# Moving two weight preparations around a layer norm in a transformer kernel on one core

## The chip, the cores and the metric

One NeuronCore of one Trainium2 chip runs the whole program. TensorE multiplies matrices into eight PSUM banks, VectorE and ScalarE evict, normalise and prepare, GpSimd does some additions and small transfers, SyncE issues the large loads. The metric is the device time of one execution in microseconds; the times given are medians of several executions.

## The reference

Three transformer layers over 512 tokens of width 1024, in float32. The first has its own form; the other two, which matter here, are

```python
def hybrid_layer(x, w_in, w_out, w_ff1, w_ff2, ...):
    proj = x @ w_in                      # queries, keys, values of two attentions, a gate
    ...                                  # forgetting attention, retention with group norm
    mix = jnp.einsum('bsc,cd->bsd', mixed, w_out)
    x = layernorm(DEEPNORM_ALPHA * x + mix, ln1_g, ln1_b)
    hid = jnp.square(jax.nn.relu(jnp.einsum('bsd,df->bsf', x, w_ff1)))
    ff = jnp.einsum('bsf,fd->bsd', hid, w_ff2)
    return layernorm(DEEPNORM_ALPHA * x + ff, ln2_g, ln2_b)
```

The layer norm needs the mean and the variance of all 1024 channels of a token, that is, all eight output tiles of `w_out` or `w_ff2`, before the first matmul of the next stage has an operand.

## The kernel before, in words

Activations lie transposed: 8 tiles of 128 channels by 512 tokens (`H`, and `P` and `Q` as operands). Each float32 operand is held as a high and a low part (`Phi`, `Plo`, `Qhi`, `Qlo` and for weights `wh`, `wl`, in further slots `wxh`, `wxl`), and each product takes three passes of TensorE: high by high (L710), high by low (L711), low by high (L713).

**Weights.** A weight matrix comes in slabs of 1 MB (SyncE, L2929) that land in two staging buffers by turns, and each slab is cut into pieces, here two of 128 output columns. Slab n may be loaded once the pieces of slab n-2 have been cut. To *prepare* a piece is one ScalarE copy to the high part (L2203, it waits for the slab to land) and one VectorE subtraction for the low part (L1301, it waits for ScalarE). Both stand in the instruction queues of these engines in program order, between evictions and norm work, so where they are placed decides what they hold up. A piece needs one of seven slots while the kernel is `wide` (four otherwise); a slot is free again when TensorE has used its piece.

The class `Walk` is run by every engine alike, so that all agree on the order. `piece(ahead, more)` takes the next piece and prepares others in advance:

```python
most = max(self.prepared + 1 + (i + 1) % 2, i + 1) + more
while self.prepared < min(i + (ahead or self.ahead) + more, len(self.weights.pieces), most) and self.ready():
    self.prepare(behind=self.behind)
```

`prepare(True)` does the high half at once and returns the low half as a function to call later.

**The stage around the change.** Behind attention and retention the output projection runs: tiles 0 and 1 together (`w.two`), 2 to 4 one by one (`w.gemm`), each evicted by VectorE into `H` (L1787, L1790), added to a running sum `accq` (L1814), and reduced by a preliminary centre `cB` (L1824), squared by ScalarE (L2586) and summed into `acc2` (L1836). Then `last_three` takes tiles 5, 6 and 7 in two halves of 256 tokens, so that the norm of the first half runs beside the matmuls of the second. Its order on TensorE: `part(0..2, 0)`, five of the eight steps of `part(0, 1)`, `mean(N, 0)` (L1038, a matmul with ones that waits for `accq` behind tile 7's first half, L1846), the rest of `part(0, 1)`, `scale(N, 0)` (L1048), `part(1, 1)`, `part(2, 1)`, and then `head`: the first four output tiles of the next stage, which need the low parts of the normalised operand (L1900). VectorE's order is written out by hand to match: per tile and half an eviction (L1859, L1862), a sum (L1846), a deviation (L1824), squares added (L1836), then `mean` (L1873), `minus` (L1880), `variance` (L1886), `times` (L1893, it needs ScalarE's reciprocal root L2610, L2612) and `lows` (L1900), in between. ScalarE has the squares, `mean` (L2603, L2605), the root, and the final scaling (L2621) with the high part (L2626).

`last_three` is called with N = 0 and N = 2 behind the output projections of the two layers, with N = 1 and N = 3 behind their feed-forward parts; the last has no next stage. It holds two places at which weights are prepared: one ahead of the third tail tile, up to three pieces in advance of use, and `fourth`, whose high half stands behind `mean(0)` and (on VectorE) `minus(0, 0, 1, 2, 3)`, and whose low half stands ahead of `times(0, 0)`.

Of the kernel before, what the change touches and what calls it, by code (L numbers as in the profile page):

```python
# [24 lines left out]
ALPHA = float(4 ** 0.25)  # L25
# [488 lines left out]
def build(nc, xT, w_in, gate_up, w_bm, w_bg, w_out, w_up, w_down, w_in2, w_out2, w_ff1, w_ff2,  # L514
          consts, params, out, vrev, cneg):
    ctx = ExitStack()
    with ctx:
# [5 lines left out]
        def signal(name):  # L523
            return Signal(ctx.enter_context(nc.semaphore(name)))
# [3 lines left out]
        w_low, vec_x, vec_attn, vec_gla, vec_ret, vec_norm = DVE = [  # L528
            signal(f"s_dve_{n}") for n in ("weight_low", "tile", "attention", "gla", "retention", "norm")]
# [163 lines left out]
        def tensor(e):  # L693
            on = Waits(e)
            w = Walk(weights, PE)
# [3 lines left out]
            def tile(hi_x, lo_x, ready):  # L699

                def step(i, c, b, k, nk, kx=None, tok=WHOLE):
                    kx = k if kx is None else kx
                    _, hi, lo = weights.tiles(i, stage, wh, wl, w.slot[i])
                    cs_ = slice(128 * c, min(128 * c + 128, weights.width(i)))
                    o = banks[b][0:cs_.stop - cs_.start, tok]
                    if k == 0:
                        on.wait_ge(w_high[i], *ready(kx), *free[b])
                    else:
                        on.wait_ge(w_high[i], *ready(kx))
                    e.matmul(o, hi[:, k, cs_], hi_x[:, kx, tok], start=k == 0, stop=False)  # L710
                    e.matmul(o, hi[:, k, cs_], lo_x[:, kx, tok], start=False, stop=False)  # L711
                    on.wait_ge(w_low[i])
                    t = e.matmul(o, lo[:, k, cs_], hi_x[:, kx, tok], start=False, stop=k == nk - 1)  # L713
                    if k == nk - 1:
                        t.then_inc(*(gemm.up("tile", i, c) if tok is WHOLE else gemm.up("half", i, tok.start // 256)))
                return step
# [63 lines left out]
            def frees(*events):  # L780

                def evict(i, c, b):
                    free[b] = [s[key + (i, c)] for s, key in events]
                return evict
# [245 lines left out]
            def norm_tile(N, j):  # L1030
                if j == 1:
                    w.beside.append(spaced([lambda: centre(N)], 3))
                    w.pace = 1.0
# [21 lines left out]
            def last_three(N, F, nxt, last_wide=False):  # L1055
                tail = [w.piece(1) for _ in range(3)]
                low = [w.next_bank() for _ in range(3)]
                high = [w.next_bank(), 6, 7]
                Q_ = tile(Qhi, Qlo, lambda k: [vec_x["hidden", F, 3, k] if N % 2 else vec_x["Q", "out", N, k]])

                def part(p, hf, ks):
                    b = (low, high)[hf][p]
                    for k in ks:
                        Q_(tail[p], 0, b, k, 8, tok=HALVES[hf])
                    if ks[-1] == 7:
                        free[b] = [vec_x["late", N, 5 + p, hf]]
                        if hf:
                            w.read_by["Q"] = tail[p]
                            w.release(tail[p])

                for _ in range(3 if nxt else 0):
                    if w.prepared < w.used + 3:
                        w.prepare()
                part(0, 0, range(8))
                part(1, 0, range(8))
                while nxt and w.prepared < w.used + 3:
                    w.prepare()
                part(2, 0, range(8))
                part(0, 1, range(5))
                mean(N, 0, (7, 0))  # L1080
                fourth = w.prepare(True) if nxt else None
                if last_wide:
                    w.narrow()
                part(0, 1, (5, 6, 7))
                scale(N, 0, (7, 0))
                if not nxt:
                    part(1, 1, range(8))
                    part(2, 1, range(8))
                    mean(N, 1, (6, 1), rest=7)
                    scale(N, 1, (6, 1), rest=7)  # L1090
                    return
                if fourth:
                    fourth()
                part(1, 1, range(8))
                part(2, 1, range(8))
                gemm.mark(("tail", N))
                four = [(w.piece(1), w.next_bank()) for _ in range(4)]

                def head(hf, ks):
                    P_ = tile(Phi, Plo, lambda k: [vec_norm["low", N, k, hf]])  # L1100
                    for k in ks:
                        for i, b in four:
                            P_(i, 0, b, k, 8, tok=HALVES[hf])

                head(0, (0, 1))
                mean(N, 1, (7, 1))
                head(0, (2, 3))
                scale(N, 1, (7, 1))
                head(0, (4, 5, 6, 7))
                w.prepare()  # L1110
                w.prepare()
                head(1, range(4))
                P_ = tile(Phi, Plo, lambda k: [vec_norm["low", N, k, 1]])
                for (i, b), ev in zip(four, nxt):
                    for k in range(4, 8):
                        P_(i, 0, b, k, 8, tok=HALVES[1])
                    gemm.mark(("tile", i, 0))
                    w.read_by["P"] = i
                    w.release(i)
                    if not last_wide or ev in nxt[:2]:  # L1120
                        ev(i, 0, b)
                for ((i, b), ev) in list(zip(four, nxt if last_wide else ()))[2:]:
                    ev(i, 0, b)
                return tile(Phi, Plo, lambda k: [vec_norm["low", N, k, 0], vec_norm["low", N, k, 1]])
# [3 lines left out]
            for L in range(2):  # L1128
# [137 lines left out]
                Qo = tile(Qhi, Qlo, lambda k: [vec_x["Q", "out", N, k]])  # L1266
# [2 lines left out]
                norm_tile(N, 0)  # L1269
                norm_tile(N, 1)  # L1270
                for j in range(2, 5):
                    w.gemm("Q", 8, Qo, frees((vec_x, ("ev",))), more=int(j == 4))
                    norm_tile(N, j)
                w.mark("hidden", F)
                Pn = last_three(N, F, [frees((act_x, ("up", F)))] * 4)
# [16 lines left out]
        def vector(e):  # L1292
# [20 lines left out]
            w = Walk(weights, DVE, low=low, sums=weight_sums)  # L1313
# [469 lines left out]
            def ev_down(j, scale=None, *events):  # L1783
                def evict(i, c, b):
                    on.wait_ge(gemm["tile", i, c], *h_over[j])
                    if scale:
                        t = e.scalar_tensor_tensor(out=H[:, j, :], in0=H[:, j, :], scalar=scale, in1=banks[b][:, :],  # L1787
                                                   op0=ALU.mult, op1=ALU.add)
                    else:
                        t = e.tensor_tensor(H[:, j, :], H[:, j, :], banks[b][:, :], ALU.add)  # L1790
                    t.then_inc(*vec_x.up("ev", i, c))
                    h_over[j] = [vec_x["ev", i, c]]
                return evict
# [56 lines left out]
            def last_three(N, F, scale, nxt, last_wide=False):  # L1850
# [54 lines left out]
                        w.prepare()  # L1905
                part(0, 0)
                part(1, 0)
                while nxt and w.prepared < w.used + 3:
                    w.prepare()
                part(2, 0)  # L1910
                add_squares(N)
                mean(0)
                minus(0, 0, 1, 2, 3)
                fourth = w.prepare(True) if nxt else None
                if last_wide:
                    w.narrow()
                part(0, 1)
# [1 line left out]
                if not nxt:  # L1919
# [18 lines left out]
                                        prm[:, V_LN2B + 14:V_LN2B + 15], ALU.mult, ALU.add)  # L1938
                    t.then_inc(*vec_norm.up("final", N, 6, 1))
                    return  # L1940
                if fourth:
                    fourth()
                times(0, 0)
                minus(0, 4)
                times(0, 1)
# [45 lines left out]
            for L in range(2):  # L1991
# [187 lines left out]
                norm_tile(N, 0)  # L2179
                norm_tile(N, 1)  # L2180
                for j in range(2, 5):
                    w.gemm("Q", 8, nothing, ev_down(j, ALPHA), more=int(j == 4))
                    norm_tile(N, j)
                w.mark("hidden", F)
                last_three(N, F, ALPHA, [ev_up(F, 0, j) for j in range(4)])
# [7 lines left out]
        def scalar(e):  # L2193
# [17 lines left out]
            w = Walk(weights, SCA, high=high)  # L2211
# [273 lines left out]
            def ev_down(j):  # L2485
                def evict(i, c, b):
                    h_over[j] = [vec_x["ev", i, c]]
                return evict
# [100 lines left out]
            def last_three(N, F, nxt, last_wide=False):  # L2589
# [4 lines left out]
                def part(p, hf):  # L2594
                    if hf:
                        w.read_by["Q"] = tail[p]
                        w.release(tail[p])
                    deviate(N, 5 + p, hf)
# [32 lines left out]
                        w.prepare()  # L2631
                part(0, 0)
                part(1, 0)
                while nxt and w.prepared < w.used + 3:
                    w.prepare()
                part(2, 0)
                mean(0)
                fourth = w.prepare(True) if nxt else None
                if last_wide:
                    w.narrow()  # L2640
                part(0, 1)
# [1 line left out]
                if not nxt:  # L2643
# [6 lines left out]
                    times(0, 5, 6, 7)  # L2650
                    times(1, 0, 1, 2, 3, 4, 5, 7)
                    return
                if fourth:
                    fourth()
                times(0, 0, 1)
                part(1, 1)
                times(0, 2)
# [21 lines left out]
            for L in range(2):  # L2679
# [131 lines left out]
                norm_tile(N, 0)  # L2811
                norm_tile(N, 1)
                for j in range(2, 5):
                    w.gemm("Q", 8, nothing, ev_down(j), more=int(j == 4))
                    norm_tile(N, j)
                w.mark("hidden", F)
                last_three(N, F, [ev_up(F, 0, j) for j in range(4)])
# [215 lines left out]
```

## Time and profile before

| | us |
|---|---|
| median of 3 runs | 2037.71 (2037.26 to 2037.96) |
| the profiled execution | 2037.82 |
| its span, first to last instruction | 2036.0 |
| TensorE busy with matmuls | 2009.3 (99%) |
| VectorE busy | 1327.5 (65%) |
| ScalarE busy | 1023.7 (50%) |
| GpSimd busy | 367.6 (18%) |
| mean granted TensorE clock | 0.998 |

The profile records one execution. Busy time counts every instruction in flight; TensorE's matmuls overlap, so 99% busy says that it seldom waited, not that it did peak work. A timeline row gives start, duration, engine, line, operation, what was written and read, the count of instructions merged into it, and in brackets how long the engine had been idle before it and which instruction released it. In the notes on SyncE's queue a load's time runs from its issue to its landing.

### The profile page before, as it was taken

Reading aid. Unit: us, or ns where it says so; the run is one execution under the profiler, and the core shown is the slowest. Engines: PE = TensorE matmul, PEld = TensorE weight load, DVE = VectorE, ACT = ScalarE, POOL = GpSimd, SP = SyncE. Lnnn points to the kernel's source line nnn. Section 1 sums busy time; section 2 is a strip of 40 time slices with the busy share of each in tenths; the row PEclk is TensorE's granted clock in tenths of the full one; section 3 lists DMA queues with packets and bytes.
Section 4 is the critical chain, followed back from the end, with each engine's and each line's share of the span. In section 5 each row is a group of like instructions: output and inputs, shape, how many; then the busy total and the mean of one; then the engine's idle time right before and its main releaser. Section 6 shows DMA issues by size and latency. Waiting matters only on the chain.

```text
span 2036.0 us, 27794 instructions
## 1 busy us (share of the span) xinstructions
PE 2009.3 (99%) x11032; PEld 1730.4 (85%) x11032; DVE 1327.5 (65%) x2095; ACT 1023.7 (50%) x1688; POOL 367.6 (18%) x315
## 2 busy tenths in 40 slices
PE   9999999999999999999999999999999999999997
PEld 6888888888898998888778899898888788899896
DVE  6765666556774665577677675567676687566576
ACT  6664344334362543466357364454566357354363
POOL 0010000000223230354000233130353000323220
PEclk9999999999999999999999999999999999999999
DMA  8332213333332323633332242332542332242431
GB/s 246 99 109 64 83 63 104 124 104 103 100 107 84 124 75 92 186 107 85 118 96 89 77 145 62 104 119 69 166 116 87 119 101 86 66 142 62 125 104 42
DMA packets 201534, 211.58 MB, mean 104 GB/s; under 512 B 7804, under 2 KB 181116, under 8 KB 201405
## 3 DMA queue, kind: packets, MB, share of 16 engines
q1 hardware_dynamic: 194544, 194.13, 30.6%
q0 software_dynamic: 6352, 15.24, 2.9%
q8 instruction: 87, 1.43, 0.3%
q10 hardware_dynamic: 508, 0.43, 0.1%
q14 instruction: 43, 0.34, 0.1%
HBM read 194.55 MB, written 8.95 MB: 100 GB/s over the span
## 4 chain that ended last, share of the span: by engine, by line
PE 90%; DVE 5%; ACT 2%; DMA 1%; issue 1%; SPq 0%; DVEq 0%; ACTq 0%
PE ps L710 19%; PE ps L713 19%; PE ps L711 19%; PE ps L766 6%; PE ps L764 6%; PE ps L762 6%; PE ps L735 2%; PE ps L738 2%; PE ps L736 2%; PE ps L817 1%; PE ps L808 1%; DVE d L1880 1%; PE ps L1227 1%; PE ps L1242 1%; PE ps L799 1%
## 5 line engine op out<-in xcount | busy, mean ns | idle before, releaser
L710 PE MATMUL ps<-Phi,wh 128*128 128x512 f32 (+1 forms) x888 | 347.4, 391 | 2.9 <-DVE Plo L1322 1.3
L1301 DVE TENSOR_TENSOR wl<-stage,wh 128x1024 fp32r<-128x1024 f32 (+1 forms) x246 | 310.4, 1267 | 37.0 <-ACT wh L2203 34.7
L713 PE MATMUL ps<-Phi,wl 128*128 128x512 f32 (+1 forms) x888 | 331.9, 374 | 0.6 <-DVE wl L1301 0.6
L711 PE MATMUL ps<-Plo,wh 128*128 128x512 f32 (+1 forms) x888 | 331.3, 373 | 0.0
L2203 ACT ACTIVATE wh<-stage 128x1024 fp32r<-128x1024 f32 (+3 forms) x249 | 248.2, 1009 | 65.5 <-PE ps L713 40.1
L710 PE MATMUL ps<-Qhi,wh 128*128 128x512 f32 (+1 forms) x664 | 252.1, 380 | 0.0
L713 PE MATMUL ps<-Qhi,wl 128*128 128x512 f32 (+1 forms) x664 | 251.8, 379 | 0.0
L711 PE MATMUL ps<-Qlo,wh 128*128 128x512 f32 (+1 forms) x664 | 251.6, 379 | 0.0
L2838 POOL TENSOR_TENSOR ws<-stage 128x1024 f32<-128x1024 f32 x20 | 55.0, 2751 | 923.1 <-PE ps L713 442.8
L710 PEld LDWEIGHTS ps<-Phi,wh 128*128 128x128 f32 x888 | 167.7, 189 | 34.3 <-DVE Plo L1900 5.1
L713 PEld LDWEIGHTS ps<-Phi,wl 128*128 128x128 f32 x888 | 167.2, 188 | 31.7 <-DVE wl L1301 1.0
L711 PEld LDWEIGHTS ps<-Plo,wh 128*128 128x128 f32 x888 | 167.8, 189 | 25.6 <-issue 1.2
L1790 DVE TENSOR_TENSOR H<-H,ps 128x512 f32<-128x512 f32 x74 | 50.8, 687 | 173.4 <-PE ps L713 173.4
L710 PE MATMUL ps<-Qhi,wxh 128*128 128x512 f32 (+1 forms) x424 | 152.5, 360 | 0.0
L711 PE MATMUL ps<-Qlo,wxh 128*128 128x512 f32 (+1 forms) x424 | 151.4, 357 | 0.0
L713 PE MATMUL ps<-Qhi,wxl 128*128 128x512 f32 (+1 forms) x424 | 151.3, 357 | 0.0
L713 PEld LDWEIGHTS ps<-Qhi,wl 128*128 128x128 f32 x664 | 124.9, 188 | 24.2 <-DVE wl L1301 0.8
L710 PEld LDWEIGHTS ps<-Qhi,wh 128*128 128x128 f32 x664 | 124.9, 188 | 23.7 <-DVE Qlo L1320 0.5
L711 PEld LDWEIGHTS ps<-Qlo,wh 128*128 128x128 f32 x664 | 124.9, 188 | 23.4
L1320 DVE TENSOR_TENSOR Qlo<-f,Qhi 128x512 fp32r<-128x512 f32 x96 | 82.3, 857 | 68.6 <-ACT Qhi L2220 68.6
L1301 DVE TENSOR_TENSOR wxl<-stage,wxh 128x1024 fp32r<-128x1024 f32 (+1 forms) x90 | 115.1, 1283 | 8.4 <-ACT wxh L2203 8.3
L2203 ACT ACTIVATE wxh<-stage 128x1024 fp32r<-128x1024 f32 (+1 forms) x90 | 85.4, 965 | 38.9 <-PE ps L713 21.7
(375 smaller groups left out, 4600.4 us busy)
## 6 DMA issues: line engine op xcount, KB each, us to landing
stage<-in_w_ff SPq DMA_DIRECT2D x64, 1024.0 KB, 5.4
stage<-in_w_in SPq DMA_DIRECT2D x39, 1024.0 KB, 5.1
stage<-in_w_up SPq DMA_DIRECT2D x16, 1024.0 KB, 5.5
stage<-in_w_down SPq DMA_DIRECT2D x16, 1024.0 KB, 4.9
stage<-in_w_in SPq DMA_DIRECT2D x30, 512.0 KB, 5.2
stage<-in_w_out SPq DMA_DIRECT2D x12, 1024.0 KB, 4.9
stage<-in_w_bg SPq DMA_DIRECT2D x4, 1024.0 KB, 4.9
vrev<-H SPq DMA_DIRECT2D x2, 2048.0 KB, 14.7
```

The costliest lines, as they stand in the source:

```text
L710: e.matmul(o, hi[:, k, cs_], hi_x[:, kx, tok], start=k == 0, stop=False)
L711: e.matmul(o, hi[:, k, cs_], lo_x[:, kx, tok], start=False, stop=False)
L713: t = e.matmul(o, lo[:, k, cs_], hi_x[:, kx, tok], start=False, stop=k == nk - 1)
L735: e.matmul(o, hi_x[:, kk, sl], hi[:, k, :], start=kk == 0, stop=False)
L762: e.matmul(o, hi[:, k0 + k, :], x, start=k == 0 and name not in again, stop=False, skip_group_check=name in again)
L764: e.matmul(o, hi[:, k0 + k, :], y, start=False, stop=False, skip_group_check=name in again)
L766: t = e.matmul(o, lo[:, k0 + k, :], x, start=False, stop=k == 3, skip_group_check=name in again)
L1301: t = e.tensor_tensor(lo, src, hi.bitcast(F32), ALU.subtract)
L1320: t = e.tensor_tensor(lo, src, hi.bitcast(F32), ALU.subtract)
L1790: t = e.tensor_tensor(H[:, j, :], H[:, j, :], banks[b][:, :], ALU.add)
L2203: e.activation(hi, src, ACT.Copy).then_inc(*w_high.up(i))
L2838: e.tensor_tensor(ws[u][:, :, :, :], one, other, ALU.add).then_inc(*pool.up("weights", i))
```

## The change

All three engines' copies of the program are changed alike. In `last_three` the weights ahead of the third tail tile are prepared up to four in advance instead of three, and `fourth` goes. In the loop over output tiles 2 to 4 behind retention, `more` is 1 for tiles 2 and 4 instead of for tile 4 alone. The diff of TensorE's copy:

```diff
@@ last_three
                 part(1, 0, range(8))
-                while nxt and w.prepared < w.used + 3:
+                while nxt and w.prepared < w.used + 4:
                     w.prepare()
                 part(2, 0, range(8))
                 part(0, 1, range(5))
                 mean(N, 0, (7, 0))
-                fourth = w.prepare(True) if nxt else None
                 if last_wide:
                     w.narrow()
...
-                if fourth:
-                    fourth()
                 part(1, 1, range(8))
...
@@ behind retention
                 for j in range(2, 5):
-                    w.gemm("Q", 8, Qo, frees((vec_x, ("ev",))), more=int(j == 4))
+                    w.gemm("Q", 8, Qo, frees((vec_x, ("ev",))), more=int(j != 3))
                     norm_tile(N, j)
```

VectorE's copy (from L1905, L1914, L1941 and L2182) and ScalarE's (from L2631, L2638, L2653 and L2814), where the same lines stand among other calls:

```diff
                 part(1, 0)
-                while nxt and w.prepared < w.used + 3:
+                while nxt and w.prepared < w.used + 4:
                     w.prepare()
                 part(2, 0)
                 add_squares(N)
                 mean(0)
                 minus(0, 0, 1, 2, 3)
-                fourth = w.prepare(True) if nxt else None
...
-                if fourth:
-                    fourth()
                 times(0, 0)
```

TensorE's copy prepares nothing itself; there the calls only keep count.

## Rows read from the trace of the kernel before

**Rows 1.** The page: busy time, share of the span and instructions of each engine.

```profile
PE 2009.3 (99%) x11032; PEld 1730.4 (85%) x11032; DVE 1327.5 (65%) x2095; ACT 1023.7 (50%) x1688; POOL 367.6 (18%) x315
```

**Rows 2.** Timeline of VectorE, place A: start us, us, what, [idle time before, releaser].

```profile
1039.17 1.23 DVE L1301 TENSOR_TENSOR wxl<-stage,wxh 128x1024 fp32r<-128x1024 f32 x1 [1.58 <-ACT wxh L2203]
...
1043.97 1.22 DVE L1301 TENSOR_TENSOR wl<-stage,wh 128x1024 fp32r<-128x1024 f32 x1 [1.65 <-ACT wh L2203]
...
1049.45 2.36 DVE L1301 TENSOR_TENSOR wl<-stage,wh 128x1024 fp32r<-128x1024 f32 x2
1053.80 1.23 DVE L1301 TENSOR_TENSOR wl<-stage,wh 128x1024 fp32r<-128x1024 f32 x1 [1.99 <-ACT wh L2203]
1054.94 0.68 DVE L1787 SCALAR_TENSOR_TENSOR H<-H,ps 128x512 f32<-128x512 f32 x1
...
1062.22 0.41 DVE L1859 SCALAR_TENSOR_TENSOR H<-H,ps 128x256 f32<-128x256 f32 x1
...
1067.44 1.22 DVE L1301 TENSOR_TENSOR wxl<-stage,wxh 128x1024 fp32r<-128x1024 f32 x1
```

**Rows 3.** Timeline of ScalarE, place A.

```profile
1052.64 1.06 ACT L2203 ACTIVATE wh<-stage 128x1024 fp32r<-128x1024 f32 x1 [2.35 <-DMA stage<-in_w_ff]
...
1061.43 0.42 ACT L2586 ACTIVATE sq<-d 128x256 f32<-128x256 f32 x1 [0.71 <-DVE d L1824]
...
1064.76 0.42 ACT L2605 ACTIVATE qB<-qB 128x256 f32<-128x256 f32 x1 [0.49 <-DVE qB L1873]
1065.08 1.05 ACT L2203 ACTIVATE wxh<-stage 128x1024 fp32r<-128x1024 f32 x1
...
1068.10 0.42 ACT L2612 ACTIVATE rB<-tB 128x256 f32<-128x256 f32 x1
```

**Rows 4.** Timeline of TensorE, place A: first half's mean, next stage's first matmul.

```profile
1063.14 0.70 PE L1038 MATMUL ps<-accq,onec 128*128 128x256 f32 x2 [2.68 <-DVE accq L1846]
...
1071.23 0.36 PE L710 MATMUL ps<-Phi,wh 128*128 128x256 f32 x1
```

**Rows 5.** SyncE's queue; loads issued in 1045:1046, 1641:1642, 1653:1654, us to landing.

```profile
1641.44 0.37 SPq L2929 DMA_DIRECT2D stage<-in_w_out  x1
...
stage<-in_w_ff SPq DMA_DIRECT2D x1, 1024.0 KB, 7.3
...
stage<-in_w_out SPq DMA_DIRECT2D x1, 1024.0 KB, 5.1
...
stage<-in_w_ff SPq DMA_DIRECT2D x1, 1024.0 KB, 5.3
```

**Rows 6.** Timeline of ScalarE, place B: square of tile 6's first half.

```profile
1405.46 0.42 ACT L2586 ACTIVATE sq<-d 128x256 f32<-128x256 f32 x1 [0.71 <-DVE d L1824]
```

**Rows 7.** Timeline of VectorE, place B: eviction of tile 7's first half.

```profile
1406.50 0.42 DVE L1862 TENSOR_TENSOR H<-H,ps 128x256 f32<-128x256 f32 x1 [0.16 <-PE ps L713]
```

**Rows 8.** Timeline of TensorE, place B: mean, next stage's first matmul.

```profile
1408.10 0.60 PE L1038 MATMUL ps<-accq,onec 128*128 128x256 f32 x2
...
1416.08 0.35 PE L710 MATMUL ps<-Phi,wh 128*128 128x256 f32 x1
```

**Rows 9.** Timeline of VectorE, place C.

```profile
1647.50 0.69 DVE L1787 SCALAR_TENSOR_TENSOR H<-H,ps 128x512 f32<-128x512 f32 x1 [1.60 <-PE ps L713]
...
1652.38 1.22 DVE L1301 TENSOR_TENSOR wl<-stage,wh 128x1024 fp32r<-128x1024 f32 x1
...
1657.84 2.36 DVE L1301 TENSOR_TENSOR wl<-stage,wh 128x1024 fp32r<-128x1024 f32 x2
...
1664.44 1.23 DVE L1301 TENSOR_TENSOR wl<-stage,wh 128x1024 fp32r<-128x1024 f32 x1
...
1668.75 0.41 DVE L1859 SCALAR_TENSOR_TENSOR H<-H,ps 128x256 f32<-128x256 f32 x1
```

**Rows 10.** Windows: PE, PEld, DVE, ACT, POOL busy (x), PEclk, DMA share, GB/s.

```profile
1063.00:1068.00 5.00, 4.86 (x37) 4.75 (x38) 4.49 (x13) 2.95 (x6) 0.00 (x0) 1.00 0.02 5
2028.00:2030.00 2.00, 0.00 (x0) 0.00 (x0) 2.00 (x8) 2.00 (x5) 0.00 (x0) 0.50 0.11 38
```

More of the change, by code:

```diff
@@ L2181, in vector @@
                 for j in range(2, 5):
-                    w.gemm("Q", 8, nothing, ev_down(j, ALPHA), more=int(j == 4))
+                    w.gemm("Q", 8, nothing, ev_down(j, ALPHA), more=int(j != 3))
                     norm_tile(N, j)
@@ L2633, in last_three @@
                 part(1, 0)
-                while nxt and w.prepared < w.used + 3:
+                while nxt and w.prepared < w.used + 4:
                     w.prepare()
@@ L2637, in last_three @@
                 mean(0)
-                fourth = w.prepare(True) if nxt else None
                 if last_wide:
@@ L2652, in last_three @@
                     return
-                if fourth:
-                    fourth()
                 times(0, 0, 1)
@@ L2813, in scalar @@
                 for j in range(2, 5):
-                    w.gemm("Q", 8, nothing, ev_down(j), more=int(j == 4))
+                    w.gemm("Q", 8, nothing, ev_down(j), more=int(j != 3))
                     norm_tile(N, j)
```

## The prediction, made before the changed kernel was run

> **What bounds the kernel now.** The page comes first: TensorE has a matmul in flight for 99% of the span [rows 1], so a weight that is cut into its halves a little earlier or later only counts where TensorE waits for it, or for something behind it. The timelines of the three places that the diff touches follow, engine by engine. They are the layer norms behind the output projection of layer 0 ("place A", 1030 to 1090 us), behind its feed-forward part ("place B", 1400 to 1436) and behind the output projection of layer 1 ("place C", 1640 to 1700). The piece numbers below count from the first piece of the output projection, 0; 5, 6 and 7 are the last three output tiles, 8 to 11 the four weights of the next stage.
>
> At A VectorE runs one long queue without rest, and what one item waits for all later ones wait for. At the fourth-last tile (j=4) it subtracts pieces 8 and 9 (the x2 row at 1049.45), then idles 1.99 us for ScalarE's high half of piece 10, and only then evicts tile 4 at 1054.94 [rows 2]. ScalarE in turn sat 2.35 us waiting for that slab to land [rows 3]. TensorE pays for it: its mean of the first half waits 2.68 us for the sum that VectorE makes right behind the eviction of tile 7's first half at 1062.22 [rows 4]. From that eviction to the next stage's first matmul pass 9.01 us (1062.22 to 1071.23) in which VectorE is hardly ever idle, so at A TensorE runs at VectorE's pace.
>
> **The change, part by part.** *Which piece goes where.* `piece()` prepares up to one piece, or two where the next piece is even, plus `more`. At A the first piece is even: j=2, 3, 4 prepare 2, 1, 3 pieces now, and 3, 1, 2 after. At C it is odd: 1, 2, 2 and one more ahead of the tail now, and 2, 2, 2 after. At both places, and at B, piece 11 moves: its high half from behind `mean(0)` and its low half from ahead of `times(0, 0)` to a spot between the second and the third tail tile. No instruction is added or removed: each low half stays 1.22 us, 1.14 us from start to the next start (1053.80 to 1054.94) [rows 2].
>
> *Place A, up to the tail.* Piece 7 joins piece 6 at j=2. Its slab is there (piece 6, of the same slab, starts at 1039.17), so evictions, sums and deviations of tiles 2 and 3 all slide by 1.14 us; TensorE doesn't wait for those, its banks come free late in any case. The slab of pieces 10 and 11 is requested when piece 7's low half ends. That was 1043.97 + 1.22 = 1045.2; it becomes 1039.17 + 1.14 + 1.22 = 1041.5, so even with the 7.3 us that this load took [rows 5] it has landed by 1048.8, before the queue reaches it. The two subtractions at j=4 then start at 1049.45 + 1.14 = 1050.59 and the eviction of tile 4 follows at 1052.87 instead of 1054.94: **2.07 us earlier**. The requests keep their order in SyncE's queue, so this one moves past nothing; GpSimd prepares no weights in these stretches.
>
> *Piece 11 in its new spot.* No row of before shows it there, so I build it from its neighbours. ScalarE makes the high half right behind the square of tile 6's first half; from a square to a high half behind it are 0.32 us (1064.76 to 1065.08), the high half takes 1.05 [rows 3], VectorE starts 0.10 after its end (1052.64 + 1.06 to 1053.80) and the next item comes 1.14 later. Sum: tile 7's eviction comes 2.61 us after the start of that square. Now it is 0.79 (1061.43 to 1062.22). The price in VectorE's queue is **1.82 us**, of which 0.7 is idle time. Bounds: 0 if another stall covered it, 1.14 if the high half were ready, 1.82 as built; not more, as the other 0.79 is there now. I take 1.82, since the order in ScalarE's queue forces it. Behind piece 11 the next slab's request is freed some 6 us sooner; its pieces are only cut behind the whole norm, so it is worth nothing. What is given back at the old spot is almost nothing: there the subtraction ended (its next start is 1067.44 + 1.14 = 1068.58) just as ScalarE's reciprocal root became ready (1068.10 + 0.42 = 1068.52), and `times(0, 0)` needs that root [rows 2, 3]. The moved work was free where it stood; without it VectorE idles a microsecond there.
>
> So A: -2.07 + 1.82 = **-0.25 us**; the wait at the mean falls from 2.68 to about 2.4.
>
> *Place B.* Nothing ahead of the tail changes, only piece 11 moves. Its slab landed long before. Square at 1405.46 [rows 6] + 2.61 = 1408.07 against 1406.50 now [rows 7]: +1.57. TensorE reaches its mean at 1408.10 without a wait [rows 8]; the sum would be ready for it 0.92 us behind the eviction (1062.22 to 1063.14 at A) [rows 2, 4], now 1407.42, after 1408.99. A wait of 0.9 us appears. Next stage's first matmul: 1408.07 + 9.01 = 1417.08 against 1416.08: **+1.0 us**. The cover of 0.57 us (9.58 us between the two now, against 9.01) is used up.
>
> *Place C.* Piece 6 moves to j=2. Its slab was requested at 1641.44 and takes 5.1 us [rows 5]: landed 1646.5, high half until 1647.6, low half, next item at 1648.8, where tile 2's eviction stands at 1647.50 now [rows 9]. VectorE's queue is late by 1.3 us from there on (the 1.60 us that it idles for TensorE before this row doesn't cover it, the slab comes too late). The slab of pieces 10 and 11 is requested at the end of piece 7's low half, 1652.38 + 1.22 = 1653.6; after the change that piece is the first of its pair at j=3 rather than the second of its pair now (1.14 sooner), in a queue that is 1.3 us late: the same instant within 0.2. With the 5.3 us that it took [rows 5] it lands at about 1659.1 and pieces 9 and 10 follow each other at j=4 without a gap. In return the subtraction at 1664.44 [rows 9], ahead of the tail, is gone: -1.14 and some 0.2 of hand-over. Net -0.05. Then piece 11: +1.82, tile 7's eviction at 1670.5 instead of 1668.75. C: **+1.75 us**, all of it as a longer wait for the mean.
>
> *Sum.* -0.25 + 1.0 + 1.75 = +2.5 us. The profiled execution took 2037.82 us (span 2036.0), 0.1 above the median of the three runs, 2037.71. I expect a span of 2038.5 and a median of **2040.2 us**, 0.12% more. A difference under 0.2% (4.1 us) is what a measurement of this kernel can't tell from none. Everything behind each place moves rigidly, as TensorE is the bound there.
>
> **Rivals.** *Faster: the stall goes and the insertion is free.* The 1.99 us stall at A is real [rows 2], and if piece 11's insertion found cover (VectorE ahead of TensorE at the third tail tile) A gives 2.07, B nothing (1407.42 is ahead of 1408.10), and C nothing or 0.05: 2035.6 us. Against it: at A and C VectorE is what TensorE waits for at just that point. The Trainium skill (DMA: Bandwidth & Descriptors, section Rules for kernel authors) advises to issue a DMA early and to wait on its semaphore late; by that rule alone this rival would hold. At A the trace agrees for the load, whose landing cost 1.99 us; but the time is then spent in VectorE's queue, of which the rule says nothing. Chance 0.12.
>
> *In between:* piece 11 costs only its 1.14 us at each place (2.0 us less in all: 2038.2), or C's 1.3 us are absorbed (2038.9), or both (2036.9). For it: the 1.60 us of idle time at C. Against it: the order of ScalarE's queue. Chance 0.18, at 2038.5.
>
> *Slower by over 0.2%: a late landing at C.* There piece 10 has no slack: its request isn't earlier, but it is wanted at j=4 rather than ahead of the tail. If that slab takes 7.3 us, as the corresponding one at A did [rows 5], it lands at 1661.0, the high half ends at 1662.0 and the low half starts at 1662.1, where 1657.84 + 1.3 + 1.14 = 1660.3 is forecast [rows 9]: all behind it is 1.8 us later, 2042.0 us. It decides from a load of some 5.5 us on. For it: one of the three loads in [rows 5] was that slow. Against it: that load was at A. Chance 0.10.
>
> *The clock.* With a late landing TensorE's wait at C would be 3.5 us longer than now. After the 2.68 us wait at A the granted clock in the window 1063 to 1068 is 1.00, the 2.4 GHz level; at the end, where TensorE has no more work, it is 0.50 [rows 10]. If it fell at C, the stretch from the mean to the next stage, 8.1 us at A (1063.14 to 1071.23) [rows 4], could take up to twice as long: up to 2050 us. The Trainium skill (TensorE: Matmul & The Clock Gate, HAM oscillation) warns that gaps between bursts of matmuls return the array to its slow clock; the trace agrees only for the end of the kernel, not for the gap at A. Chance 0.02.
>
> That the change does nothing: the same piece would have to find no free slot at its new spot; tile 4's slot is free by then. The loop would not end otherwise. No chance worth a number.
>
> **How the numbers follow.** Forecast 0.58, in between 0.18, faster rival 0.12, late landing 0.10, clock 0.02. All but the last two lie within 0.2% of 2037.71 (2033.6 to 2041.8). Faster by over 0.2% needs more than all of A's wait and C's together: 0.02. Within: 0.87. Slower: 0.11. The forecast's own range is 2039 to 2041.5. The range 2035.5 to 2042.3 takes in the in-between cases (from 2036.9), the faster rival (2035.6), since without it and the late landing 0.24 would be left out, and the late landing (2042.0); only the clock and what nobody thought of stay out.
>
> **What would show it.** Right: at A no idle time of VectorE for ScalarE's high half at j=4, a mean's wait of about 2.4 us; at B a new wait of 0.9 us at the mean; at C a wait there 1.75 us longer than now; VectorE idle for some 0.7 us ahead of piece 11's low half and for a microsecond ahead of `times(0, 0)`, three times each. Wrong: a wait at A under 1 us (insertion covered), none at B, or at C an idle VectorE that waits for a landing.

## The result, and the profile after

| | before | after |
|---|---|---|
| median of 21 runs, us | 2037.60 (2035.79 to 2038.44) | **2040.83** (2039.91 to 2042.57) |
| profiled execution, us | 2037.82 | 2040.88 |
| its span, us | 2036.0 | 2039.1 |
| mean granted TensorE clock | 0.998 | 0.997 |

The ratio is 1.0016, 95% interval 1.0011 to 1.0022: 3.2 us more, within the 0.2% that was called no change, and 0.6 us above the forecast of 2040.2. The executed work is the same; TensorE's share of busy time is again 99% and doesn't show where the time went. The profile's line of busy times, which answers to [rows 1]:

```profile
PE 2010.6 (99%) x11032; PEld 1731.6 (85%) x11032; DVE 1327.4 (65%) x2095; ACT 1023.6 (50%) x1688; POOL 367.1 (18%) x315
```

The waits of TensorE that end on VectorE's sum `accq` (us in total, times, longest), first before, then after:

```profile
PE ps L1038 <- DVE accq L1846: 3.6, 2, 2.7
```

```profile
PE ps L1038 <- DVE accq L1843: 5.7, 3, 2.7
```

Two waits became three. Before, they were 2.68 us at A [rows 4] and 0.90 at C, where TensorE's row is

```profile
1669.68 0.70 PE L1038 MATMUL ps<-accq,onec 128*128 128x256 f32 x2 [0.90 <-DVE accq L1846]
```

After, they are 2.38 at A, 0.66 at B and 2.68 at C. Timeline of VectorE after, place A, answering to [rows 2] (three fewer lines stand above it, so L1301 is L1298, L1787 is L1784, L1859 is L1856, L1893 is L1890):

```profile
1039.25 1.22 DVE L1298 TENSOR_TENSOR wxl<-stage,wxh 128x1024 fp32r<-128x1024 f32 x1 [1.62 <-ACT wxh L2197]
1040.39 1.22 DVE L1298 TENSOR_TENSOR wl<-stage,wh 128x1024 fp32r<-128x1024 f32 x1
...
1050.65 2.36 DVE L1298 TENSOR_TENSOR wl<-stage,wh 128x1024 fp32r<-128x1024 f32 x2
1052.93 0.68 DVE L1784 SCALAR_TENSOR_TENSOR H<-H,ps 128x512 f32<-128x512 f32 x1
...
1060.81 1.23 DVE L1298 TENSOR_TENSOR wxl<-stage,wxh 128x1024 fp32r<-128x1024 f32 x1 [0.52 <-ACT wxh L2197]
1061.95 0.41 DVE L1856 SCALAR_TENSOR_TENSOR H<-H,ps 128x256 f32<-128x256 f32 x1
...
1068.29 0.43 DVE L1890 TENSOR_TENSOR d<-d,rB 128x256 f32<-128x256 f32 x1 [1.02 <-ACT rB L2606]
```

Piece 7 follows piece 6 at once, and at j=4 the two subtractions run into the eviction of tile 4 (1052.93, forecast 1052.87) with no idle time: the 1.99 us are gone. Piece 11 stands ahead of tile 7's eviction (1061.95, forecast 1061.97). The last row is the old spot: VectorE now idles there for the root. TensorE's rows at A, answering to [rows 4]: the wait is 0.30 shorter, and the next stage begins 0.29 us sooner (forecast 0.25).

```profile
1062.88 0.70 PE L1038 MATMUL ps<-accq,onec 128*128 128x256 f32 x2 [2.38 <-DVE accq L1843]
...
1070.94 0.36 PE L710 MATMUL ps<-Phi,wh 128*128 128x256 f32 x1
```

Place B, VectorE, answering to [rows 7]:

```profile
1406.54 1.23 DVE L1298 TENSOR_TENSOR wl<-stage,wh 128x1024 fp32r<-128x1024 f32 x1 [0.52 <-ACT wh L2197]
1407.68 0.41 DVE L1859 TENSOR_TENSOR H<-H,ps 128x256 f32<-128x256 f32 x1
```

Place B, TensorE, answering to [rows 8]:

```profile
1408.61 0.70 PE L1038 MATMUL ps<-accq,onec 128*128 128x256 f32 x2 [0.66 <-DVE accq L1843]
...
1416.67 0.35 PE L710 MATMUL ps<-Phi,wh 128*128 128x256 f32 x1
```

The kernel arrives at B 0.3 us early, so in its own time the eviction is 1.18 + 0.3 = 1.5 us later, and the next stage 0.59 + 0.3 = 0.9 us. Place C, VectorE, answering to [rows 9]:

```profile
1648.46 1.23 DVE L1298 TENSOR_TENSOR wxl<-stage,wxh 128x1024 fp32r<-128x1024 f32 x1 [1.74 <-ACT wxh L2197]
1649.60 0.68 DVE L1784 SCALAR_TENSOR_TENSOR H<-H,ps 128x512 f32<-128x512 f32 x1
...
1661.18 1.23 DVE L1298 TENSOR_TENSOR wl<-stage,wh 128x1024 fp32r<-128x1024 f32 x1 [0.17 <-ACT wh L2197]
1662.32 0.68 DVE L1784 SCALAR_TENSOR_TENSOR H<-H,ps 128x512 f32<-128x512 f32 x1
...
1670.20 1.23 DVE L1298 TENSOR_TENSOR wxl<-stage,wxh 128x1024 fp32r<-128x1024 f32 x1 [0.52 <-ACT wxh L2197]
1671.35 0.41 DVE L1856 SCALAR_TENSOR_TENSOR H<-H,ps 128x256 f32<-128x256 f32 x1
...
1673.95 0.42 DVE L1870 TENSOR_TENSOR qB<-muB,cB 128x256 f32<-128x256 f32 x1 [0.49 <-ACT muB L2597]
```

The kernel enters C 0.82 us late. Tile 2's eviction is 1649.60 - 1647.50 - 0.82 = 1.28 us late in its own time (forecast 1.3), tile 7's 1671.35 - 1668.75 - 0.82 = 1.78 (forecast 1.75). VectorE's queue did what was forecast of it. The last row is new: 0.49 us of idle time for `muB`, ScalarE's copy of the mean. Its cause stands in TensorE's rows there:

```profile
1672.27 1.22 PE L1038 MATMUL ps<-accq,onec 128*128 128x256 f32 x2 [2.68 <-DVE accq L1843]
```

The mean takes 1.22 us where it took 0.70 before. The windows around it (PE, PEld, DVE, ACT, POOL, then PEclk, DMA share, GB/s), of after; before, each of them has 1.00:

```profile
1672.00:1673.00 1.00, 0.73 (x3) 0.64 (x3) 0.55 (x2) 0.41 (x1) 0.00 (x0) 0.58 0.35 70
1673.00:1674.00 1.00, 1.00 (x6) 0.91 (x5) 0.48 (x2) 0.39 (x2) 0.00 (x0) 0.50 0.84 201
1674.00:1675.00 1.00, 1.00 (x6) 1.00 (x6) 1.00 (x4) 0.42 (x1) 0.00 (x0) 0.50 0.96 292
1675.00:1676.00 1.00, 1.00 (x6) 0.91 (x6) 1.00 (x4) 0.00 (x0) 0.00 (x0) 0.71 1.09 389
```

TensorE's clock was at its lower level, 1.2 GHz, for some 3.4 us behind the wait; from 1676 on it is 1.00 again. C cost 1.78 + 0.49 = 2.27 us; read from the shifts in the table below it is 2.26.

### The profile page after: what moved, and what is told of

The parts are those of the page before. It is cut to its first block, busy times and chain, and to the rows that moved or that the text cites. A ratio compares the mean times of both kernels' runs of the same rounds, so it can differ in the third digit from the quotient of the medians.

```text
span 2039.1 us, 27794 instructions
## 1 busy us (share of the span) xinstructions
PE 2010.6 (99%) x11032; PEld 1731.6 (85%) x11032; DVE 1327.4 (65%) x2095; ACT 1023.6 (50%) x1688; POOL 367.1 (18%) x315
## 4 chain that ended last, share of the span: by engine, by line
PE 89%; DVE 5%; ACT 3%; DMA 1%; issue 1%; SPq 0%; DVEq 0%; ACTq 0%
PE ps L710 19%; PE ps L713 19%; PE ps L711 19%; PE ps L766 6%; PE ps L764 6%; PE ps L762 6%; PE ps L735 2%; PE ps L738 2%; PE ps L736 2%; PE ps L817 1%; PE ps L808 1%; DVE d L1877 1%; PE ps L1224 1%; PE ps L1239 1%; PE ps L799 1%
## 5 line engine op out<-in xcount | busy, mean ns | idle before, releaser
L1298 DVE TENSOR_TENSOR wl<-stage,wh 128x1024 fp32r<-128x1024 f32 (+1 forms) x246 | 310.1, 1266 | 35.6 <-ACT wh L2197 33.6
L1787 DVE TENSOR_TENSOR H<-H,ps 128x512 f32<-128x512 f32 x74 | 50.8, 686 | 174.9 <-PE ps L713 174.8
L1298 DVE TENSOR_TENSOR wxl<-stage,wxh 128x1024 fp32r<-128x1024 f32 (+1 forms) x90 | 115.1, 1283 | 9.4 <-ACT wxh L2197 9.3
```

The costliest lines, as they stand in the source:

```text
L1298: t = e.tensor_tensor(lo, src, hi.bitcast(F32), ALU.subtract)
```

## The experiments

All kernels but the fillers' one compute the same operations in another order. Where the time is gained and lost is read from ScalarE's rows: the shift of each against the same row of the profiled execution of before, the median of nine in a row, in us. A place costs the difference of two neighbouring columns. The table has all experiments; they follow one by one.

| kernel | median us (runs) | entering A | behind A | behind B | entering C | behind C |
|---|---|---|---|---|---|---|
| the change | 2040.83 (21) | 0.05 | -0.31 | 0.58 | 0.82 | 3.08 |
| e1, extra weight alone | **2036.03** (11) | 0.11 | -1.82 | -1.82 | -1.72 | -1.75 |
| e2, move alone | 2043.52 (8) | -0.14 | 0.16 | 1.06 | 1.07 | 3.33 |
| e3, extra weight in layer 0 | 2036.05 (11) | -0.22 | -2.44 | -2.45 | -1.69 | -1.71 |
| e4, high half sooner | 2039.02 (11) | 0.08 | -0.74 | -0.31 | -0.14 | 0.93 |
| e5, move at B alone | 2038.68 (11) | -0.18 | -0.51 | 0.38 | 0.91 | 0.88 |
| e6, fillers at C | 2040.32 (11) | -0.04 | 0.04 | 0.94 | 1.01 | 2.72 |
| e7, move alone again | 2042.19 (1) | -0.10 | 1.62 | 2.51 | 2.68 | 4.38 |
| e8, before again | 2037.45 (1) | 0.00 | -0.22 | -0.24 | -0.30 | -0.34 |

**e1, the extra weight alone.** From the change, the move undone in all three engines' copies:

```diff
-                while nxt and w.prepared < w.used + 4:
+                while nxt and w.prepared < w.used + 3:
                     w.prepare()
...
+                fourth = w.prepare(True) if nxt else None
...
+                if fourth:
+                    fourth()
```

> One part alone: the weight that is prepared at the third output tile is kept, the move of the fourth is undone (its high half again behind the mean, its low half behind the wait). My theory (the extra piece takes a VectorE stall of 2.07 us away at A, and is worth nothing at C): 2.1 us less than before, about 2035.5 us, the wait of the mean's matmul at A down from 2.68 to about 0.6 us, at B unchanged, at C unchanged or up by at most 0.1, and the clock at C at 1.00. The rival (the extra piece itself makes VectorE late at C, by its 1.3 us behind a slab that lands late, and gives nothing at A): 2037.6 to 2039 us. If both are right at once, A gains 2.1 and C loses 1.3: 2036.8 us.

2036.03 us (2035.38 to 2036.50) against 2037.71 for before beside it; the ratio is 0.9993, interval 0.9984 to 1.0001, so the gain of 1.7 us is at the edge of what this measurement tells from none, though all 11 runs lie below 26 of the 30 of before. The gain is all at A: 1.93 us (0.11 to -1.82). VectorE there:

```profile
1050.86 2.36 DVE L1301 TENSOR_TENSOR wl<-stage,wh 128x1024 fp32r<-128x1024 f32 x2
1053.14 0.68 DVE L1787 SCALAR_TENSOR_TENSOR H<-H,ps 128x512 f32<-128x512 f32 x1
...
1060.41 0.42 DVE L1859 SCALAR_TENSOR_TENSOR H<-H,ps 128x256 f32<-128x256 f32 x1
```

TensorE at A: the wait is 0.77 us instead of 2.68 (0.6 expected).

```profile
1061.34 0.70 PE L1038 MATMUL ps<-accq,onec 128*128 128x256 f32 x2 [0.77 <-DVE accq L1846]
```

At C the kernel loses and wins nothing (-1.72 to -1.75; forecast -0.05), with a wait of 0.89 us and a clock of 1.00. The rival, that the extra weight itself costs at C, falls. From tile 4's to tile 7's eviction are 1060.41 - 1053.14 = 7.27 us here and 1061.95 - 1052.93 = 9.02 with the change: the moved piece costs 1.75 us of VectorE's queue (forecast 1.82).

**e3, the extra weight in layer 0 alone.** As e1, and

```diff
-                    w.gemm("Q", 8, Qo, frees((vec_x, ("ev",))), more=int(j != 3))
+                    w.gemm("Q", 8, Qo, frees((vec_x, ("ev",))), more=int(j == 4 or (L == 0 and j == 2)))
```

> The extra weight at the third output tile in layer 0 alone (place A), the move undone. My theory: A gives 2.07 us and C is as before, so 2035.5 us, the same as with the extra weight in both layers within 0.2 us. The rival (the extra piece costs at C what it is queued behind, 1.3 us): this kernel is 1.1 to 1.3 us faster than the one with it in both layers.

2036.05 us (2035.69 to 2037.00), ratio 0.9992 (0.9984 to 1.0001): the same as e1. A gave 2.22 us here (-0.22 to -2.44), of which 0.76 were lost again between B and C (see e5). The extra weight in layer 1 is worth nothing, and costs nothing.

**e2 and e7, the move alone.** From the change:

```diff
-                    w.gemm("Q", 8, Qo, frees((vec_x, ("ev",))), more=int(j != 3))
+                    w.gemm("Q", 8, Qo, frees((vec_x, ("ev",))), more=int(j == 4))
```

> The other part alone: the fourth is moved ahead of the last tail tile, the extra weight at the third output tile is left out. My theory (the move costs 1.8 us at A, 0.9 at B, 1.8 at C, and the extra piece is what pays A's back): 4.5 us more than before, 2042.1 us, with the wait of the mean's matmul at A at about 4.5 us, at B 0.7, at C 2.7; where the clock falls in a wait, up to 0.5 us more for each such place, so up to 2043.1. The rival (the two parts only work together, the pieces prepared early are what makes the move dear): 2038 to 2039.5 us.

2043.52 us (2041.08 to 2044.96), ratio 1.0027 (1.0017 to 1.0038). The move costs 5.8 us by the medians; 4.5 were expected, up to 1.0 more for the clock. B took 0.90 (0.16 to 1.06) and C 2.26 (1.07 to 3.33), as with the change, so the extra weight has no part in either. But A took only 0.30 in the profiled execution, at 2041.16 us, where 1.8 was expected, and TensorE's wait there was 2.78 us, not 4.5. The runs fell apart into 2 near 2041.1 and 6 from 2042.5 up. So it was profiled once more:

> The kernel with the move alone once more, for its profile: its runs fell into two groups, 2041.1 us (2 of 8) and 2042.5 to 2045.0 (6 of 8), and the execution shown so far is of the first. The theory (the slab of feed-forward weights that is issued at 1045.3 us lands in 5.5 us in the first group and in 7.3 us in the second, as in the kernel before): with 3 chances in 4 a run of 2043 to 2044 us, and then VectorE idle for about 2 us behind the high half at the last full output tile, where the first group has 0.30. The rival (the second group is of the clock alone): a run of the second group has that idle time at 0.3 us and a clock that falls at more places.

It took 2042.19 us, in neither of the two groups, where 2043 to 2044 had been expected with 3 chances in 4. The load of the slab of pieces 10 and 11 (us from issue to landing: least, median, longest), and VectorE's timeline row with what it idled for the high half at j=4. In e2:

```profile
DMA to landing us min/median/max: 5.6/5.6/5.6
```

```profile
1051.99 1.23 DVE L1298 TENSOR_TENSOR wl<-stage,wh 128x1024 fp32r<-128x1024 f32 x1 [0.30 <-ACT wh L2197]
```

In e7:

```profile
DMA to landing us min/median/max: 6.9/6.9/6.9
```

```profile
1053.40 1.23 DVE L1298 TENSOR_TENSOR wl<-stage,wh 128x1024 fp32r<-128x1024 f32 x1 [1.59 <-ACT wh L2197]
```

The stall follows the landing to the tenth: 1.3 us later, 1.29 us more idle time, and A cost 1.72 instead of 0.30. Of the 0.13 that is left, the clock explains about half (0.31 in e7 against 0.25 in e2, by how much more the shift grows between 1055 and 1075 than with the change). The 0.30 of e2 is then the piece's 1.75 and the clock's 0.25, less the 1.69 by which its stall is shorter than the 1.99 of before.

What sets the two groups apart is not shown by this. No execution of the slower one was profiled, and a landing as late as in before (0.4 us more than e7's) and a fall of the clock at C (0.55) would bring e7 to some 2043.1 us, an estimate; five of the eight runs took 2043.42 to 2044.96. Their mean granted clocks are 0.995 and 0.996, against 0.997 and 0.998 in the other three, so the clock has a part in it that no profile here shows.

**e8, the kernel before once more.**

> The kernel before once more, for its profile: 5 of its 30 runs took 2035.9 to 2036.4 us, the others 2037 to 2038.4. The theory (the same slab lands on time in the few and late in the many): a run near 2037.7 us with the slab's landing at 7 us or more and VectorE idle for about 2 us at the last full output tile of A, or a run near 2036.1 us with the landing at 5.5 us and hardly any idle time there. The rival (the groups differ in something else): the landing and the time do not go together.

2037.45 us. That is a run of the many, with a landing and an idle time somewhat below what was expected for it. Its load and VectorE's row, answering to [rows 5] (7.3 us) and [rows 2] (1.99):

```profile
DMA to landing us min/median/max: 6.8/6.8/6.8
```

```profile
1053.39 1.22 DVE L1301 TENSOR_TENSOR wl<-stage,wh 128x1024 fp32r<-128x1024 f32 x1 [1.49 <-ACT wh L2203]
```

Across all executions that have this wait the two go together: 5.6 us and 0.30 (e2), 6.8 and 1.49 (e8), 6.8 and 1.52 (e5), 6.9 and 1.59 (e7), 7.3 and 1.99 (before). That the few shortest runs of before (4 of 30 at 2035.9 to 2036.4; the expectation says 5) are those with a landing in time fits their distance of about 1.5 us from the others, but none of them was profiled, so it is argued and not shown.

**e4, the high half sooner.** From the change, piece 11 between the tail tiles, split over two spots:

```diff
                 part(0, 0)
+                fourth = w.prepare(True) if nxt else None
                 part(1, 0)
-                while nxt and w.prepared < w.used + 4:
-                    w.prepare()
+                if fourth:
+                    fourth()
                 part(2, 0)
```

> The whole change, but the moved fourth is split: its high half is made on ScalarE behind the first tail tile, its low half on VectorE behind the second, so that VectorE no longer idles for the high half between them. My theory (of the 1.8 us that the moved low half costs in VectorE's queue, 1.14 is its own time and 0.7 idle time for the high half): 0.7 us less at A, at B and at C than with the change, so up to 2.1 us less, 2038.7 us; at C the wait of the mean falls to about 2.0 us, and the clock there may stay at 1.00, 0.5 us more. The rival (the idle time comes of ScalarE being behind with its squares anyway): within 0.4 us of the change, 2040.4 to 2041.2 us.

2039.02 us (2038.54 to 2039.45), ratio 1.0007 (0.9998 to 1.0016), so 1.8 us less than the change (up to 2.1 expected). VectorE at A:

```profile
1052.97 0.68 DVE L1785 SCALAR_TENSOR_TENSOR H<-H,ps 128x512 f32<-128x512 f32 x1
...
1060.04 0.43 DVE L1834 TENSOR_TENSOR acc<-acc,sq 128x256 f32<-128x256 f32 x1 [0.28 <-ACT sq L2582]
1060.38 1.22 DVE L1299 TENSOR_TENSOR wxl<-stage,wxh 128x1024 fp32r<-128x1024 f32 x1
1061.52 0.41 DVE L1857 SCALAR_TENSOR_TENSOR H<-H,ps 128x256 f32<-128x256 f32 x1
```

The 0.52 us for the high half are gone, but 0.28 for the square behind it came in their place. It saved 0.46 at A (-0.82 against -0.36), 0.46 at B and 1.19 at C; at C the wait is 2.01 us and the clock stays at 1.00, which is 0.49 of it. So of the 1.75 us some 0.5 to 0.7 came of the order of ScalarE's queue. The rest is the low half itself, and it still isn't worth its place: e1 is 3 us faster.

**e5, the move at B alone**, made from the kernel before:

```diff
-                while nxt and w.prepared < w.used + 3:
+                while nxt and w.prepared < w.used + (4 if N == 1 else 3):
                     w.prepare()
...
-                fourth = w.prepare(True) if nxt else None
+                fourth = w.prepare(True) if nxt and N != 1 else None
```

> The move at one place alone, B, where no extra weight is prepared: the kernel before with the fourth ahead of the last tail tile behind layer 0's feed-forward, and nothing else changed. My theory (1.57 us more in VectorE's queue, a wait of about 0.7 us at the mean's matmul where there was none): 0.9 us more at B, 0.9 to 1.0 us more in the end, 2038.6 us against 2037.7. The rival (what is lost at B is taken back by the slack of layer 1's retention, where VectorE idles for transfers): no difference at the end, within 0.3 us.

2038.68 us (2038.18 to 2039.54) against 2037.72, ratio 1.0005 (0.9996 to 1.0014): 0.96 us by the medians, too little for the interval to tell from none. B itself is read from the trace: 0.89 us (-0.51 to 0.38), with a wait of 0.66. Layer 1's retention doesn't take it back; it added 0.5 of its own, between B and C. There GpSimd waits twice in a row for small transfers, and how long varies from execution to execution. The first of the two waits, in before and in e3:

```profile
1457.68 1.14 POOL L2884 DMA_DIRECT2D x_Cb<-cneg  x2 [3.16 <-DMA cneg<-x_z]
```

```profile
1456.98 1.14 POOL L2884 DMA_DIRECT2D x_Cb<-cneg  x2 [4.91 <-DMA cneg<-x_z]
```

The second, in before and in e5:

```profile
1462.71 0.60 POOL L2900 TENSOR_SCALAR x_bi<-x_Cb,stat 128x128 f32<-128x128 f32 x1 [3.89 <-DMA x_Cb<-cneg]
```

```profile
1463.64 0.60 POOL L2900 TENSOR_SCALAR x_bi<-x_Cb,stat 128x128 f32<-128x128 f32 x1 [4.22 <-DMA x_Cb<-cneg]
```

Both waits together are 7.05 us in before, 7.16 with the change, 7.60 in e5 and 7.73 in e3; between B and C the last three lost 0.24, 0.53 and 0.76 us against before. In the other six executions the sum is 6.98 to 7.13 and the loss -0.06 to 0.17. The two go together, which fits the transfers as the cause, but no run changed the transfers. This also is noise that a single profile brings into such a sum.

**e6, fillers ahead of the mean at C.** The change, with 18 matmuls more whose product is never read:

```diff
+                if N == 2:
+                    on.wait_ge(*free[5])
+                    for _ in range(18):
+                        e.matmul(banks[5][:, 0:256], onecr[:, :], Qhi[:, 0, 0:256], start=True, stop=True)
                 mean(N, 0, (7, 0))
```

> The whole change, with 18 more matmuls of 128 by 256 (about 2.2 us of TensorE, their product is never read) ahead of the mean's matmul at C, so that TensorE does not idle there. The theory (the 2.7 us wait lets the clock fall to 0.5 for 3.4 us, and that costs 0.5 us through the mean, ScalarE's copy of it and VectorE): the granted clock stays at 1.00 from 1665 to 1680 us, muB's row begins 0.4 to 0.5 us earlier behind the mean's last addition, and the time is 0.5 us less than with the change, 2040.3 us. The rival (the clock falls for what TensorE does elsewhere, or its fall is hidden behind VectorE): no difference in time within 0.2 us, or a clock that falls as before.

2040.32 us (2039.90 to 2041.78), 0.51 less than the change; ratio to before 1.0014 (1.0005 to 1.0023). The gap of 0.5 us lies inside the intervals of the two ratios; the trace shows its place. TensorE at C:

```profile
1669.62 2.32 PE L1083 MATMUL ps<-Qhi,onec 128*128 128x256 f32 x18
1672.43 0.70 PE L1038 MATMUL ps<-accq,onec 128*128 128x256 f32 x2 [0.49 <-DVE accq L1847]
```

ScalarE there:

```profile
1673.16 0.39 ACT L2601 ACTIVATE muB<-ps 128x256 f32<-128x256 f32 x1
```

The granted clock is 1.00 from 1664 to 1680, the mean takes 0.70 us, and `muB` comes 0.73 us behind the mean's start, against 1.26 with the change (1672.27 to 1673.53). C cost 1.71 us (1.01 to 2.72), against 2.26. In this same execution the clock fell at A, untouched, and took some 0.2 us.

The experiment does not show that the fillers kept the clock up. In e7 there are none, the wait at C is 2.64 us, and the clock stayed at 1.00 too. What the four executions do show together is the price of the fall: C cost 2.26 in both with it (the change, e2) and 1.70 and 1.71 in both without (e7, e6).

## Why the prediction was right, and where it was off

*What bounds.* Right. The time went into waits of TensorE for VectorE's sum at the three places; between the places the change's shift moves by no more than 0.24 us.

*The stall at A.* Forecast -2.07, shown by e1 as -1.93, by e3 as -2.22 and by the change's eviction of tile 4 as -2.01 (1054.94 to 1052.93). The mechanism was right. What the forecast didn't see is that the stall is no constant of the kernel: it was read from one execution in which the load took 7.3 us, the longest of five. With a load of 5.6 us it is 0.30 us. The extra weight is an insurance against a late landing, not a fixed gain. Beside a run of before that had its slab in time, the 0.3 us that A gained with the change would have been a loss of about 1.3 us (an estimate: 1.99 - 0.30 - 0.36).

*Piece 11's price.* Forecast 1.82 at each place; 1.75 at A, 1.5 in VectorE's queue at B (forecast 1.57), 1.78 net at C (forecast 1.75). The neighbours' rows were enough to build it, though no row showed it. Of the forecast 0.7 us of idle time 0.52 is visible as such, at all three places; at C another 0.15 us stands ahead of the sum of squares before it.

*B's cover.* Forecast +1.0 behind a cover of 0.57; 0.90 with the change, 0.91 in e2, 0.89 in e5. The new wait itself is 0.66 us, where 0.9 was forecast.

*The old spot.* 1.02 us of idle time for the root where the low half had stood, three times, as forecast. The work was free there.

*C.* VectorE's queue as forecast, and the wait went from 0.90 to 2.68 us, 1.78 longer; e1 and e3 show the extra weight's share to be nothing within 0.05. The late landing, the rival on the slower side, was not in this trace: the load took 5.4 us, ScalarE waited 0.26 us for that slab and VectorE 0.17. In all ten profiled executions this load took 5.3 to 5.5 us. Whether the change's three runs at 2042.3 to 2042.6 were late landings was not seen; two of them have the lowest mean clock of the 21, 0.996.

*The step that failed.* The clock. The prediction gave its fall at C a chance of 0.02, and only together with a late landing; it fell with none, behind a wait of 2.68 us, in the one profiled execution of the change, and in one of the two of the move alone. And it was priced at up to 8 us, "up to twice as long" for the stretch from the mean to the next stage. It cost 0.49: the lower level lasted 3.4 us, and in that stretch VectorE sets the pace, so that the slow matmuls held it up only through the one copy `muB`. At 1675.6 TensorE was 4.1 us behind the same matmul of before, at 1684.8 only 3.1. Forecast +2.5, measured in spans +3.1; of the 0.6 between them the clock is 0.49 and the transfers between B and C 0.24, less some 0.2 by which A and B came out better. The Trainium skill (TensorE: Matmul & The Clock Gate, HAM oscillation) warned of gaps between bursts; the trace of the change agrees at C and still not at A.

*The rule on DMA* (the Trainium skill, DMA: Bandwidth & Descriptors, Rules for kernel authors) advises to issue a transfer early and to wait for it late. The runs agree at A: there the load is issued 3.6 us sooner (1041.72 for 1045.30) and the stall is gone, and this is all that helped. e1 is that part without the move, and with e3 it is the fastest kernel here.

## What to carry to other kernels

Preparation that passes from one engine to another belongs where the second one waits anyway, as ahead of `times`, where VectorE waits for the reciprocal root. Moved to a point at which a third engine waits for that queue, as at A and C, it costs its whole length plus the hand-over (1.14 + 0.6 us here), even if its data are there; where there was slack, as at B, it costs what the slack doesn't cover (0.9).

A change made of two parts should be timed as two. Here one gains 1.7 us, and the other costs 4.8 on top of it (2040.83 against 2036.03). Alone it costs 5.8 (2043.52 against 2037.71): the parts don't simply add up, and the missing microsecond is not explained here.

A stall read from one execution that ends on a DMA should be read from several before it is counted as a gain.

## What was not expected of the hardware

*The clock and the length of a wait.* TensorE's wait ahead of the mean, and the granted clock in the 7 us behind it, over all profiled executions, where the wait was over 1 us:

| clock 1.00 | clock 0.76 |
|---|---|
| 1.92 (e4 A), 2.01 (e4 C), 2.38 (change A), 2.39 (e5 A), 2.64 (e7 C), 2.68 (before A) | 2.28 (e8 A), 2.57 (e6 A), 2.65 (e2 C), 2.68 (change C), 2.78 (e2 A), 4.14 (e7 A) |

Windows of the change, A and C:

```profile
1063.00:1070.00 7.00, 7.00 (x56) 6.89 (x57) 5.43 (x16) 3.70 (x9) 0.00 (x0) 1.00 0.53 153
1672.00:1679.00 7.00, 6.73 (x40) 6.46 (x41) 4.97 (x15) 2.82 (x7) 0.00 (x0) 0.76 0.50 150
```

The same two windows of the kernel before, run again (e8):

```profile
1063.00:1070.00 7.00, 7.00 (x44) 6.77 (x44) 6.32 (x17) 4.78 (x10) 0.00 (x0) 0.76 0.09 16
1672.00:1679.00 7.00, 6.86 (x58) 6.69 (x57) 6.83 (x18) 4.75 (x11) 0.00 (x0) 1.00 0.38 111
```

With waits of 2.3 to 2.7 us the clock falls or not, and not by their length; every fall has 0.76 in its 7 us, so about the same 3.4 us at the lower level. The kernel before has it too, at A, in one of its two profiled executions. It costs 0.2 to 0.3 us at A and 0.55 at C. No fall was seen behind a wait of under 1 us at these places.

*The landing time of one load.* The same 1 MB load, issued at the same point (1045.2 to 1045.4), landed in 5.6, 6.8, 6.8, 6.9 and 7.3 us. In the five kernels with the extra weight, which issue it at 1041.3 to 1041.9, it took 5.4 or 5.5 us each time. So the sooner issue did not only hide the landing: it also came with a shorter load. Windows of the kernel before around its landing (the last column is GB/s):

```profile
1049.00:1050.00 1.00, 1.00 (x7) 0.84 (x6) 0.86 (x2) 1.00 (x2) 0.00 (x0) 1.00 1.08 383
1050.00:1051.00 1.00, 1.00 (x11) 1.00 (x10) 1.00 (x2) 0.29 (x1) 0.00 (x0) 1.00 0.19 56
1051.00:1052.00 1.00, 1.00 (x10) 1.00 (x10) 0.81 (x1) 0.00 (x0) 0.00 (x0) 1.00 0.07 13
1052.00:1053.00 1.00, 1.00 (x11) 1.00 (x10) 0.00 (x0) 0.36 (x1) 0.00 (x0) 1.00 0.03 8
```

Some 990 KB had come between 1046 and 1050 (the sum of the four windows from 1046), so nearly all of the slab, and ScalarE waited until 1052.6 for the rest. Why the last bytes come late, and why only at the later point of issue, was not tried.
